# Sums of squares in four norms: three GpSimd adds and three TensorE sums in place of eight TensorE sums

## The reference

```python
def rms_norm(x, gain):
    xf = x.astype(jnp.float32)
    y = xf * lax.rsqrt(jnp.mean(xf * xf, axis=-1, keepdims=True) + EPS)
    return (y * gain.astype(jnp.float32)).astype(x.dtype)

def modulate(x, gain, shift, scale):
    return rms_norm(x, gain) * (1 + scale[:, None, :]) + shift[:, None, :]

def second_block(...):
    for i in range(DEPTH_2):
        ...
        h = modulate(x, norm_mix[i], sh_m, sc_m)
        y = moba_attention(h, ...) if i % N_MIXERS == 0 else short_conv(h, ...)
        x = x + g_m[:, None, :] * y
        h = modulate(x, norm_ffn[i], sh_f, sc_f)
        x = x + g_f[:, None, :] * swiglu(h, w_gate_up[i], w_down[i])
```

## Time and profile before

| | before |
|---|---|
| median of three runs | 934.43 us (933.42 to 934.47) |
| the profiled execution | 935.05 us, of which its span 933.4 us |
| mean granted TensorE clock | 0.996 |
| TensorE busy | 911.7 us (98%) |
| VectorE busy | 760.3 us (81%) |
| ScalarE busy | 491.6 us (53%) |
| GpSimd busy | 49.7 us (5%) |
| DMA | 207.66 MB, mean 222 GB/s |

### The profile page before, as it was taken

How to read it: one execution, slowest core, us unless ns; L and a number is a source line. 1 busy time by engine, 2 the same in 40 slices (tenths; PEclk the granted TensorE clock), 3 DMA queues, 4 the chain that set the end, 5 groups by cost and what they waited for, 6 DMA issues and landing times.

```text
span 933.4 us, 18366 instructions
## 1 busy us (share of the span) xinstructions
PE 911.7 (98%) x7367; PEld 884.2 (95%) x7367; DVE 760.3 (81%) x1058; ACT 491.6 (53%) x749; POOL 49.7 (5%) x87
## 2 busy tenths in 40 slices
PE   9999999999999999899999999999899999999998
PEld 8999999999999988898999999999899999999786
DVE  5999989988899788898897777887999896667444
ACT  6346657666574355654564444436444564544431
POOL 5100000000001000010000010010000000000000
PEclk9999999999999999999999999999999999999999
DMA  9787475556659826565478888894577557765531
GB/s 297 255 285 256 137 251 196 186 181 224 224 199 373 286 91 227 180 226 180 138 230 296 284 287 295 310 331 137 184 253 265 193 182 246 251 223 180 181 135 46
DMA packets 132125, 207.66 MB, mean 222 GB/s; under 512 B 4710, under 2 KB 109536, under 8 KB 126944
## 3 DMA queue, kind: packets, MB, share of 16 engines
q1 hardware_dynamic: 123968, 156.47, 50.5%
q0 software_dynamic: 8064, 50.34, 15.4%
q10 hardware_dynamic: 32, 0.01, 0.0%
HBM read 205.75 MB, written 1.05 MB: 222 GB/s over the span
## 4 chain that ended last, share of the span: by engine, by line
PE 76%; DVE 16%; ACT 4%; issue 3%; DMA 1%; ACTq 0%; DVEq 0%; SPq 0%
PE bank L1644 21%; PE bank L1646 21%; PE bank L1645 21%; DVE w_lo L960 5%; DVE ada_acc L976 2%; PE bank L1796 2%; ACT w_hi L569 1%; PE bank L1715 1%; PE bank L1713 1%; PE bank L1724 1%; DVE conv L1112 1%; PE bank L1689 1%; DVE scr L994 1%; PE bank L1681 1%; PE bank L1683 1%
## 5 line engine op out<-in xcount | busy, mean ns | idle before, releaser
L960 DVE TENSOR_TENSOR w_lo<-w_raw,w_hi 128x1024 fp32r<-128x1024 f32 x294 | 352.4, 1220 | 97.7 <-ACT w_hi L569 96.3
L569 ACT ACTIVATE w_hi<-w_raw 128x1024 fp32r<-128x1024 f32 x294 | 304.5, 1055 | 216.2 <-PE bank L1646 203.3
L1644 PE MATMUL bank<-act_hi,w_hi 128*128 128x256 f32 x1312 | 368.0, 281 | 4.9 <-DVEq L1617 3.9
L1646 PE MATMUL bank<-act_hi,w_lo 128*128 128x256 f32 x1312 | 364.3, 278 | 0.0
L1645 PE MATMUL bank<-act_lo,w_hi 128*128 128x256 f32 x1312 | 364.2, 278 | 0.0
L1644 PEld LDWEIGHTS bank<-act_hi,w_hi 128*128 128x128 f32 x1312 | 247.7, 189 | 6.7 <-DVEq L1617 4.5
L1645 PEld LDWEIGHTS bank<-act_lo,w_hi 128*128 128x128 f32 x1312 | 247.4, 189 | 0.4 <-issue 0.2
L1646 PEld LDWEIGHTS bank<-act_hi,w_lo 128*128 128x128 f32 x1312 | 247.3, 188 | 0.0
L976 DVE SCALAR_TENSOR_TENSOR ada_acc<-ada_raw,silu_c,ada_acc 128x2048 f32<-128x2048 f32 (+1 forms) x56 | 114.3, 2041 | 5.0 <-DMA ada_raw<-in_w_ada 4.1
L1644 PE MATMUL bank<-hid_hi,w_hi 128*128 (+1 forms) x352 | 98.6, 280 | 0.3 <-DVE w_lo L960 0.3
L1645 PE MATMUL bank<-hid_lo,w_hi 128*128 (+1 forms) x352 | 97.4, 277 | 0.0
(11 more groups left out here) (307 smaller groups left out, 1390.8 us busy)
## 6 DMA issues: line engine op xcount, KB each, us to landing
w_raw<-in_w_gate_up SPq DMA_DIRECT2D x44, 1024.0 KB, 5.1
ada_raw<-in_w_ada POOLq DMA_DIRECT2D x40, 1024.0 KB, 5.4
w_raw<-in_w_down SPq DMA_DIRECT2D x33, 1024.0 KB, 5.1
w_raw<-in_w_in SPq DMA_DIRECT2D x23, 1024.0 KB, 7.3
w_raw<-in_w_up SPq DMA_DIRECT2D x22, 1024.0 KB, 5.3
w_raw<-in_w_qkv SPq DMA_DIRECT2D x12, 1024.0 KB, 6.3
w_raw<-in_w_out SPq DMA_DIRECT2D x8, 1024.0 KB, 7.1
ada_raw<-in_w_ada POOLq DMA_DIRECT2D x16, 512.0 KB, 5.1
```

The source lines that it names most:

```text
L569: act.activation(unit(w_hi, u), raw_half(c, h), ACT.Copy).then_inc(hi_ready, 1)
L960: dve.tensor_tensor(unit(w_lo, u), raw_half(c, h), unit(w_hi, u).bitcast(F32), ALU.subtract).then_inc(lo_ready, 1)
L1644: pe.matmul(dst, a_hi, b_hi, start=start, stop=False, skip_group_check=True)
L1646: return pe.matmul(dst, a_lo, b_hi, start=False, stop=stop, skip_group_check=True)
```

## The change

In norms 1, 3, 4 and 5, GpSimd adds tiles 2 and 3 of the squares onto tiles 0 and 1, then tiles 4 and 5, and at last tile 1 onto tile 0. TensorE sums that one tile over the partitions, then tiles 6 and 7: three matmuls in place of eight, all of them behind the third tile of `raw_chunk`. The pairs that lay in `output_chunk`, in `down_layer` of norm 4 and behind the first tile of its `raw_chunk` are gone. Norm 2 keeps its eight sums. A new semaphore, `sq_folded`, orders the adds and tells TensorE. GpSimd's loop of fetches is written out, so that the adds can stand behind the fetch of step 11, 25, 41 and 49.

```diff
+SUMS_AFTER = {11: 1, 25: 3, 41: 4, 49: 5}
+SUMMED = {1: 1, 3: 2, 4: 3, 5: 4}
...
+            def fold_squares(n):
+
+                done = 3 * (SUMMED[n] - 1)
+                for j in (1, 2):
+                    pool.wait_ge(sq_ready, 5 * (n - 1) + j + 1)
+                    if j == 2:
+                        pool.wait_ge(sq_folded, done + 1)
+                    pool.tensor_tensor(scr[:, 0:2, :], scr[:, 0:2, :], scr[:, 2 * j:2 * j + 2, :], ALU.add
+                                       ).then_inc(sq_folded, 1)
+                pool.wait_ge(sq_folded, done + 2)
+                pool.tensor_tensor(scr[:, 0, :], scr[:, 0, :], scr[:, 1, :], ALU.add).then_inc(sq_folded, 1)
+
             for n, (l, s, left, width) in enumerate(SECTIONS):
-                def fetch(j, i=None):
-
-                    pool.dma_start(ada_raw[:, j, 0:width], w_ada_2[l][cols(j * P, 2 * P, i, P), s * ADA_W + left:s * ADA_W + left + width]
+                def fetch(j, i=0):
+
+                    row = (2 * i + j) * P
+                    pool.dma_start(ada_raw[:, j, 0:width], w_ada_2[l][row:row + P, s * ADA_W + left:s * ADA_W + left + width]
                                    ).then_inc(ada_landed[j], 16)
...
-                with pool.Fori(int(n == 0), 4) as i:
-                    for j in range(2):
-                        pool.wait_ge(ada_used, at(8 * n + j - 1, 2, i))
-                        fetch(j, i)
+                for step in range(8 * n + (2 if n == 0 else 0), 8 * n + 8):
+                    pool.wait_ge(ada_used, step - 1)
+                    fetch(step % 2, step % 8 // 2)
+                    if step in SUMS_AFTER:
+                        fold_squares(SUMS_AFTER[step])
...
@@ raw_chunk
-                    if arrives and n == 4 and k == 0:
-                        square_part(4, 2)
                     if arrives and k == 2:
-                        square_rest(n, 3)
+                        folded_squares(n)
...
@@ output_chunk
-                        if n == 3 and outputs[0] == 2 and r < 1:
-                            square_part(NORM_AFTER[c0], r + 2)
...
             def square_part(n, part):
 
-                if n == 2 and part == 0:
+                if part == 0:
                     pe.wait_ge(both_ready, KT)
                 pe.wait_ge(sq_ready, 5 * (n - 1) + part + 1)
                 for k in (2 * part, 2 * part + 1) if part < 3 else (part + 3,):
-                    w = both_gain[:, k, :] if n == 2 else ones[:]
-                    ins = pe.matmul(bank[SUM_BANK[n]][:, 0:T], w, scr[:, k, :], start=k == 0, stop=k == KT - 1)
+                    ins = pe.matmul(bank[SUM_BANK[n]][:, 0:T], both_gain[:, k, :], scr[:, k, :], start=k == 0, stop=k == KT - 1)
                 if part == 4:
                     ins.then_inc(ss_ready, 1)
+
+            def folded_squares(n):
+
+                pe.wait_ge(sq_folded, 3 * SUMMED[n])
+                pe.matmul(bank[SUM_BANK[n]][:, 0:T], ones[:], scr[:, 0, :], start=True, stop=False)
+                for k in (6, 7):
+                    pe.wait_ge(sq_ready, 5 * (n - 1) + k - 2)
+                    ins = pe.matmul(bank[SUM_BANK[n]][:, 0:T], ones[:], scr[:, k, :], start=False, stop=k == 7)
+                ins.then_inc(ss_ready, 1)
...
@@ down_layer
-                    if (h, j) in ((0, 3), (1, 2)):
-                        square_part(NORM_AFTER[c0], h)
+                    if c0 == DOWN1 and (h, j) in ((0, 3), (1, 2)):
+                        square_part(2, h)
```

More of the change, by code:

```diff
@@ L277, in model_kernel @@
         sq_ready = sem("sq_ready")
+        sq_folded = sem("sq_folded")
         ss_ready = sem("ss_ready")
```

## The result

| | before | after |
|---|---|---|
| median | 934.45 us (933.42 to 934.94, four runs) | 946.62 us (945.31 to 951.34, four runs) |
| ratio | | 1.0141, 95% interval 1.0118 to 1.0164 |
| profiled execution | 935.05 us, span 933.4 us | 951.34 us, span 949.6 us |
| mean granted TensorE clock | 0.996 | 0.987 |

The change costs 12.2 us by the medians. The sign was right and the time lies in the range; the forecast of +6.8 us was about half of it. Medians are of runs in the fast state, from which one run in this document fell out (e8, 946.40 us).

A forecast was written before the change was run, and what follows sets the result against it. TensorE carries 76% of the chain, with VectorE 0.24 us behind it in norm 1. Adds and VectorE taking turns cost +2.3, +2.1, +2.0 and +0.4, sum +6.8 us on 934.43: 941.2; range 932.3 to 948.

The forecast's parts named there:

- What is late next: Norms 1, 3, 5: VectorE's addition of tiles 6 and 7 limits TensorE's relief to 0.47, 0.41 and 0.51 us.
- 24 records of sums: Sign in the four norms: 24 records of sums with the ones matrix in place of 64.
- The sign of a gap of over 4 us: Norm 1, if there is a lock: TensorE has a gap of over 4 us before the folded sum.
- The price of the adds: GpSimd's three adds: 1.17 us for each large one, 0.65 for the small one, 3.0 us a norm.
- The ends of my bounds: GpSimd's adds: 0.65 and 0.39 us if operands come at once, 1.69 and 0.91 if the write takes its turn too.
- What the adds do to VectorE: They take turns: norms 1, 3, 5 and 4 cost +2.3, +2.1, +2.0 and +0.4 us; chance 0.40.
- The row at 14.02: VectorE's 128x2 instruction took 0.60 us, not about 0.15, ending with GpSimd's memset; chosen for each add's whole length over no delay.
- The other row: Two `w_lo` pieces beside a 1.83 us memset took 2.51 us, normally 2.35: no such holding back of VectorE.
- VectorE keeps its turn: Rival: GpSimd's second and third adds wait for gapless VectorE work; 13.4 us slower, 947.8; chance 0.22.
- the forecast's 0.70: From the last square to TensorE's next large matmul: semaphore 0.05, start 0.10, one sum 0.43, pitch 0.12 us.
- Norm 4 and the loop: Norm 4: +0.4 us, the third add letting one `raw_lo` go first; GpSimd's written-out fetches cost nothing.
- TensorE has no gaps behind the norms: Behind the norms: TensorE has no gaps, so the gains of norms 1, 3 and 5, 1.4 us, last.

The follow-up runs named there:

- e8: e7, with VectorE adding tiles 6 and 7 ahead of three `raw_lo` and one `w_lo` in norms 1, 3 and 5: 940.10 us, ratio 1.0036.
- e2: The changed kernel without GpSimd's adds; three sums that leave out five of eight tiles: 934.02 us, ratio 1.0002.
- e7: The kernel before, with the four norms' ones and squares in fp32r, so a sum is one pass; no GpSimd adds: 932.38 us, ratio 0.9983.
- e4: e3 with each GpSimd add replaced by a memset of 1024, 1024 and 512 columns: 934.85 us, ratio 1.0012.
- e3: The kernel before with fetches written out and the three adds into an unused spare tile, all eight sums kept: 940.95 us, ratio 1.0072.
- e5: e4 with each memset replaced by a copy from `scr` into the spare tile, one input: 941.39 us, ratio 1.006.
- e9: The changed kernel with filler matmuls on TensorE in norms 3 to 5, none in norm 1: 945.70 us, ratio 1.0129.
- e10: The kernel of e6 once more, filler matmuls in all four norms of the changed kernel: 943.57 us, ratio 1.0091.
- e1: The kernel before with only GpSimd's fetches written out, eight sums and no adds: 933.82 us, ratio 0.999.
- e6: The changed kernel with filler matmuls in TensorE's gap and the folded sum moved behind them: 944.28 us, ratio 1.0124.

## Why the prediction was right or wrong, point by point

- **What is late next.** Right. TensorE's relief ends at VectorE: e2 gave 0.46, 0.37 and 0.45 us in norms 1, 3 and 5 where the forecast had 0.47, 0.41 and 0.51, and e7 shows the same limit. The counts came as named: 24 records of sums in the four norms. The sign of a gap of over 4 us before the folded sum was misnamed: that sum waits for the adds alone and came at 143.28, inside the gap.
- **The price of the adds.** A little low. The first alone takes 1.29 us and the third 0.79 to 0.81 (forecast 1.17 and 0.65), so 3.4 us a norm and not 3.0. The ends of my bounds (0.65 and 1.69 for the large ones) were far off. The Trainium skill (GPSIMD Engine Reference, 3.1) gives 4497 ns for 2048 columns, by columns an estimate of 1.12 and 0.56: the large add is 15% above that here, the small one 40%.
- **What the adds do to VectorE.** Right, and it decided the sign. The first `w_lo` was 1.00 us longer (forecast 0.96). The three `raw_lo` were 1.5 longer, where I put 1.82 for the second and third add; part of them fits between. Tiles 6 and 7 came 2.2 us late (144.96 less 142.88, and the 0.1 by which this execution runs ahead there); by the forecast it would have been 2.78 less the 0.24 of idle time saved, 2.5. The row at 14.02, on which I chose between the two bounds, led to the right one by luck. GpSimd only writes there, and VectorE's instruction reads one tile, while e4 shows that a GpSimd that only writes does not hold up an instruction with two inputs. So what held the instruction at 14.02 is a different case, and no run explains it. The other row, the `w_lo` beside a memset, was no evidence against the forecast for the same reason. The sentence in front that the engines meet only at semaphores is too strong: VectorE and GpSimd also meet at SBUF. The Trainium skill (SBUF — State Buffer, SBUF: two separate sides) has the lock, and with e3, e4 and e5 the runs agree with it: an add or a copy on GpSimd holds back a two-input instruction of VectorE until it has ended, a memset does not.
- **VectorE keeps its turn (the rival).** Wrong. The second add ended 1.1 us behind the `w_lo` beside it, although VectorE's next instruction was ready. Its forecast of 947.8 is close to 946.6 by chance: the third add ended before tiles 6 and 7, not after five more `raw_lo`.
- **The step that failed: what stands behind the gap.** I had named a gap of over 4 us in TensorE, and counted it as waiting time alone. I took the matmuls behind it at their old duration. They ran at 0.50 of the clock. For norm 1: the last square ends at 146.15, and with the forecast's 0.70 TensorE would be back at 146.85 in place of 145.02, +1.8 us. From there to the `raw_lo` matmuls of `raw_chunk` it took 2.18 us before (145.02 to 147.20), which gives 149.03; they begin at 151.74. The missing 2.7 us are the clock. In the sum, e3 has the contention without the gap: +6.6 us, against +6.8 forecast. After has 5.6 us on top. e9 against e10 shows 2.2 us of it in norm 1 to hang on the filling of the gap, and norms 3, 5 and IN3 differ between after and e10 by 1.1, 1.1 and 1.3 (norm 5 by TensorE's own delay). By medians, e10 takes 3.7 us off the change, and 1.3 more if its own third sum behind the gap is counted: about 5 of the 5.6 us. The intervals of the two kernels, some 2 us either way each, leave that loose. The traces say the same: after is 7.3 above e3 and 5.7 above e10, which with the 1.3 makes 7.0 of 7.3.
- **Norm 4 and the loop.** Norm 4 was forecast at +0.4 and gave +0.18. The written-out loop cost nothing (e1). That TensorE has no gaps behind the norms, so that gains last, is wrong behind norm 4: TensorE waits 2.81 us in IN3 of before, and e2 lost its gain of norm 4 there.

**What stays open.** In IN3, 30 us behind norm 4, TensorE waits some 3 us for VectorE's queue (2.81 in before, 3.01 in e1, e3, e10 and after). In before, e1 and e6 the granted clock stays at 1.00 behind this wait; in e3, e9 and e10 it falls to 0.50 for 3.4 us, and in e2 and after for 6.8. The wait itself does not tell them apart (2.82 in e6, 2.83 in e9), and I can't say what decides it. What IN3 costs goes with the length of the fall: 0.0 us in e6, 0.6 in e3, e9 and e10, 1.7 in e2 and 1.9 in after. So of the clock's share the part in the norms is shown by fillers put in and left out, and the part in IN3 (1.3) is only seen.

## What to carry to other kernels

Moving work onto an idle GpSimd is not free while VectorE is near the chain with two-input instructions from SBUF: count every GpSimd instruction that reads SBUF at up to its whole length on VectorE as well (here 2.5 us of 3.4 a norm); memsets cost such instructions nothing (e4). Work taken off TensorE turns into a gap if another engine is right behind it, and a gap of some 4 us cost more than itself here, because TensorE came back at half the clock: either fill it or leave the work where it is. Before a relief is priced, look for the second engine's idle time at the same place; here it was 0.24 us in norm 1, and e2 won 0.46 there out of 2.6 us of work.

## What the runs showed of the hardware that I had not expected

**Half the clock after a gap that one matmul breaks.** In after and e9 the gap in norm 1 runs from 141.9 (e9: 141.5) to 145.9, with one sum in it, and the clock is at 0.50 for 6.8 us in all, the last 5.5 of them with TensorE at work. In norm 3 of after the two idle stretches are 1.65 and 1.96 us, and the clock falls for 3.4. In e3, whose gap in norm 1 is 1.44 us, and e2, whose sums lie closer (1.06 us idle), it stays at 1.00 there. The length of one gap does not decide it alone: in the attention of before the clock falls at 355.5 and 396.5 us, each time behind an idle stretch of only some 1.6 us.

**Two paces of the large matmuls at the full clock.** With a granted clock of 1.00 in the records, they follow each other either every 113.3 ns or every 117.8 ns, and can hold one of them for tens of microseconds. Three rows of TensorE's timeline of e6, with 18 steps between the first and the last:

```profile
146.48 0.28 PE L1732 MATMUL bank<-raw_hi,w_lo 128*128 128x256 f32 x1
146.60 0.28 PE L1730 MATMUL bank<-raw_hi,w_hi 128*128 128x256 f32 x1
...
148.60 0.28 PE L1732 MATMUL bank<-raw_hi,w_lo 128*128 128x256 f32 x1
```

And of e3, also with 18 steps:

```profile
146.47 0.28 PE L1735 MATMUL bank<-raw_hi,w_lo 128*128 128x256 f32 x1
146.59 0.28 PE L1733 MATMUL bank<-raw_hi,w_hi 128*128 128x256 f32 x1
...
148.52 0.28 PE L1735 MATMUL bank<-raw_hi,w_lo 128*128 128x256 f32 x1
```

2.12 us against 2.05. The slower pace ran in before from 221 to 281 and from 705 to 755 us, in after from 684 to 732 and 767 to 880, in e5 and e6 from 146 to 258, in e8 from 659 to 725 and 740 to 860. It changes where the flow of matmuls is disturbed. 100 us of it cost nearly 4 us, so the 160 us of after would account for the 6 us by which its profiled execution lies above its two fastest, and the pace may be behind most of the spread between executions; that is not shown, as the others have no trace. What sets it no run here tells. It is also why a median over few executions of this kernel can't settle a microsecond, while the growth of a delay across one norm can.
